# A gated HGRN2 and S5 block on one core: the small matmuls of an S5 slot gathered in one group

## The chip, the cores and the metric

The kernel runs on one core of a Trainium2 chip. The metric is the device time of one execution in microseconds, as the median of several runs. The names of the engines are those of the profile: PE is TensorE (its weight loads are PEld), DVE is VectorE, ACT is ScalarE, POOL is GpSimd, and SP issues DMAs.

## What is computed

Input x is 2048 tokens of 1024 channels. `u = RMSNorm(x)` is projected to eight parts. Two mixers run beside each other, gates merge them, and a second gated projection and a last norm follow. The S5 mixer, cut to its core:

```python
# 32 groups of 16 channels, each with 64 complex states
xr = einsum('bsgc,gnc->bsgn', u, bbr);  xi = einsum('bsgc,gnc->bsgn', u, bbi)
hr, hi = associative_scan(lam * h + x)             # over the sequence
y  = C_re hr - C_im hi + d * u
ys = gelu(y); ys = glu_a * sigmoid(glu_b) * silu(z)
h += W_out(sigmoid(gate_hg) * y_hg + sigmoid(gate_s5) * y_s5)
h += (p @ W_ple) * sigmoid(RMSNorm(h) @ W_ple_gate)
return RMSNorm(h)
```

## The kernel before

Three parts follow each other on every engine: the head (norm, the projections of HGRN2 and its mixer), the S5 part (`part_s5`) and the tail (`part_tail`). Every large product is made of three float32r matmuls (`split_matmuls`, L107 to L109): weights and activations are each split in a rounded value and the rest, by ACT (the rounding) and DVE (the difference). `u_hi` and `u_lo` stay in SBUF.

The S5 part has NB = 20 slots. In slot b, PE projects weight block b over four token tiles (`project`, 8 x 3 matmuls of 512 columns for each tile). The first four blocks are z slots: DVE multiplies each drained tile (`gated`). The other blocks are gates, drained by a sigmoid on ACT. POOL stores the tiles. Beside this, slots 2 to 17 hold the S5 work of one pair of groups each, p = b - 2.

The S5 work of a pair cuts the sequence in 256 chunks of 8 tokens. `matrices` (DVE) builds bb, X and Z. PE turns X through bank `px` (transposes, L1123), and ACT copies the result to `w_in_t` (L1192). PE makes the taps, the response within a chunk, from bb and Z (L1127); DVE's `taps` copies them to `msb`, and SP spreads them by eight DMAs in `w_intra` (L1053). PE makes the inputs of each chunk from `w_in_t` and U into `pin` (L1138). DVE's `angles` and ACT's Sin make the rotations, and DVE's `states` rotates the inputs, scans them and writes `Hp`. Last, PE makes the outputs from `w_intra` and U (L1146), and from Z and Hp (L1150), into `py`; ACT's `gelu` drains them, and POOL's `store_y` writes them to memory. Within a slot PE has transposes and taps inside the second tile of the projection, the inputs inside the third tile, and the outputs behind the fourth. All these small matmuls are plain float32; they have two records each in the profile, the transposes one.

Engines run their instructions in order, with semaphore waits written out by hand. DVE's order in a slot is `matrices`, `angles`, (z: `gated` 0), the difference of the next slot's weights (L1212), `taps`, (`gated` 1), `states`, (`gated` 2 and 3). ACT's order is `gelu` of the pair before, Sin, the copy to `w_in_t`, and the four drains, with the rounding of the next weights (L1164) behind the first. SP's order is weights, U of the next pair (behind the outputs of the pair before), and the eight copies of the taps.

The tail has the sections glu, os5, ohg, out, ple and pgate, in units of one weight load. Blocks go round six PSUM banks. Two means of squares are needed for each token tile: DVE adds eight squares in `sumsq` [128, 512] (L1892), and one float32 matmul with ones adds them over the partitions (`mean_square`, L1663), behind the first unit of glu, and behind that of os5. `one_over_rms` on ACT follows. In the last tile there is only the first of these, inside ple, and the very last mean is made in two halves (L1738). The head has such a matmul too, but in float32r (L479): it first adds the upper 64 partitions to the lower ones, and puts the rounded sum in the lower half of `osq_parts` and the rest in the upper half.

Of the kernel before, what the change touches and what calls it, by code (L numbers as in the profile page):

```python
# [18 lines left out]
ds = bass.ds  # L19
# [100 lines left out]
def part_head(nc, c, a, w, banks, xs, u_hi, u_lo):  # L120
# [9 lines left out]
    with Bufs(nc, "hg") as m:  # L130
# [818 lines left out]
        return Part(sync, gpsimd, tensor, scalar, vector, drained=[(sigf, STEPS), (sg_done, STEPS), (iv_staged, 2 * TOKENS), (qe_done, STEPS)],  # L949
# [3 lines left out]
def part_s5(nc, c, a, w, banks, u_hi, u_lo, drained, head_over):  # L953
# [11 lines left out]
    with Bufs(nc, "s5") as m:  # L965
# [19 lines left out]
        Z = m.sb("Z", [P, 2, SC + 1, GC])  # L985
# [10 lines left out]
        ps, py, px, pin = banks[0:NT], banks[4:6], banks[6], banks[7]  # L996
# [10 lines left out]
        def slots(engine, body):  # L1007
# [6 lines left out]
            for b in range(PAIRS, NB):  # L1014
                body(b, b - AHEAD if b < PAIRS + AHEAD else None, b % 2, False)
# [3 lines left out]
        def sync(sp):  # L1019
# [13 lines left out]
            def body(b, p, r, z):  # L1033
# [12 lines left out]
                if not is_at(p, 0):  # L1046
                    sp.wait_ge(y_done, p)
                if not isinstance(p, int) or p + 1 < PAIRS:
                    load_u(p + 1, 1 - r)
                sp.wait_ge(msb_done, p * 2 + 2)  # L1050
                for j in range(SC):
                    rows = slice(j * GC, (j + 1) * GC)
                    sp.dma_start(w_intra[rows, r, :, j * GC:P], msb[:, :, 0:SC - j].rearrange("c q j d -> c q (j d)")  # L1053
                                 ).then_inc(intra_in, 16)
# [3 lines left out]
        def gpsimd(pool):  # L1058
# [19 lines left out]
            def body(b, p, r, z):  # L1078
                if is_at(b, 1):
                    constants()  # L1080
                if p is not None and not is_at(p, 0):
                    store_y(p - 1, 1 - r)
                elif is_at(b, PAIRS + AHEAD):
                    store_y(PAIRS - 1, 1)
                for t in range(NT):
# [8 lines left out]
        def tensor(pe, last_step):  # L1094
# [13 lines left out]
            def body(b, p, r, z):  # L1108
                pe.wait_ge(w_lo_done, b + (W0 + 1))
                first = is_at(p, 0)  # L1110
                if p is None:
                    for t in range(NT):
                        project(b, r, t)
                        if is_at(b, 0):
                            last_step(t)
                    return
                project(b, r, 0)
                project(b, r, 1, range(0, 3))
                if not first:
# [12 lines left out]
                pe.wait_ge(turned_done, p + 1)  # L1132
                pe.wait_ge(u_in[r], (p // 2) * 32 + 32 if isinstance(p, int) else (p - r) * 16 + 32)
                if not first:
                    pe.wait_ge(hp_done, p)
                for k in range(2):
                    for q in range(2):
                        ins = pe.matmul(pin[q * NS:(q + 1) * NS, k * NCK:(k + 1) * NCK], w_in_t[:, k, q * NS:(q + 1) * NS],  # L1138
                                        U[:, r, q], start=True, stop=True)
                ins.then_inc(pin_done, 1)  # L1140
                project(b, r, 2, range(2, KT))
                project(b, r, 3)
                pe.wait_ge(intra_in, (p + 1) * 16 * SC)
# [990 lines left out]
```

## Time and profile before

| | |
|---|---|
| median of 3 runs | 2202.24 us (2201.95 to 2203.3) |
| the profiled execution: its own time | 2201.22 us |
| its span | 2199.6 us |
| granted TensorE clock, mean | 0.998 |
| busy: PE, PEld | 2182.7 us (99%), 1782.0 us (81%) |
| busy: DVE, ACT, POOL | 1371.7 us (62%), 941.7 us (43%), 148.2 us (7%) |
| PE's longest waits | 1.8 us (L1738), 1.7 us (L380), 1.6 us (L107 at the start), 0.6 us (L1123) |

The span runs from the first to the last instruction of one execution. A matmul of 512 columns in float32r has a record of 0.39 us, but the next one starts 0.23 us after it: the records overlap, and what a matmul costs is read from the distance of starts.

### The profile page before, as it was taken

What the parts mean: (1) busy time and instruction counts of PE and PEld (TensorE: products, weight loads), DVE (VectorE), ACT (ScalarE), POOL (GpSimd) and SP (SyncE); (2) the same over time, 40 slices, a digit from 0 to 9 for tenths busy, and PEclk for the clock granted to TensorE, in tenths of its full rate; (3) what the DMA queues carried; (4) which work ended last, traced back from release to release, by engine and by line L of the source; (5) the groups of instructions that cost most, each with busy time, mean ns of one, the idle gap of its engine ahead of it and who ended that gap; (6) DMA issues with size and microseconds to landing.
All of it is one profiled execution on the core that took longest, in us unless ns stands there. A gap on an engine that the chain in (4) does not pass through costs nothing.

```text
span 2199.6 us, 29498 instructions
## 1 busy us (share of the span) xinstructions
PE 2182.7 (99%) x10488; PEld 1782.0 (81%) x10488; DVE 1371.7 (62%) x2788; ACT 941.7 (43%) x1381; POOL 148.2 (7%) x268
## 2 busy tenths in 40 slices
PE   9999999999999999999999999999999999999997
PEld 7788888888888888887777777888888888888886
DVE  7700058778778778757666566266567566665756
ACT  6511145545545555533333333243444354354345
POOL 0000000000000000011111111111002001200100
PEclk9999999999999999999999999999999999999999
DMA  6422111111111111022222222376347536634632
GB/s 220 105 72 67 48 63 58 37 41 57 42 39 53 43 38 43 25 92 85 82 83 88 85 85 80 95 225 187 116 123 244 169 97 189 226 111 128 226 116 77
DMA packets 140092, 223.25 MB, mean 101 GB/s; under 512 B 38816, under 2 KB 82592, under 8 KB 140000
## 3 DMA queue, kind: packets, MB, share of 16 engines
q1 hardware_dynamic: 119920, 160.39, 24.2%
q0 software_dynamic: 20080, 61.64, 8.0%
q8 instruction: 57, 0.93, 0.2%
q14 instruction: 35, 0.29, 0.0%
HBM read 166.25 MB, written 54.53 MB: 100 GB/s over the span
## 4 chain that ended last, share of the span: by engine, by line
PE 96%; DVE 2%; ACT 1%; DMA 1%; issue 0%; SPq 0%; DVEq 0%; ACTq 0%
PE c_bank L107 30%; PE c_bank L108 29%; PE c_bank L109 29%; PE c_bank L474 1%; PE c_bank L451 1%; PE c_bank L461 1%; PE c_bank L472 1%; PE c_bank L1150 1%; PE c_bank L1138 1%; PE c_bank L1146 1%; PE c_bank L1127 0%; PE c_bank L479 0%; DMA x_xs<-x_in 0%; PE c_bank L1663 0%; DVE x_xs L824 0%
## 5 line engine op out<-in xcount | busy, mean ns | idle before, releaser
L107 PE MATMUL c_bank<-u_hi,c_w_both 128*128 128x512 f32 x1216 | 487.0, 400 | 2.8 <-DVE c_w_both L880 1.6
L109 PE MATMUL c_bank<-u_hi,c_w_both 128*128 128x512 f32 x1216 | 473.5, 389 | 0.0
L108 PE MATMUL c_bank<-u_lo,c_w_both 128*128 128x512 f32 x1200 | 468.3, 390 | 0.0
L107 PEld LDWEIGHTS c_bank<-u_hi,c_w_both 128*128 128x128 f32 x1216 | 228.3, 188 | 71.6 <-issue 20.6
L109 PEld LDWEIGHTS c_bank<-u_hi,c_w_both 128*128 128x128 f32 x1216 | 228.3, 188 | 48.8
L108 PEld LDWEIGHTS c_bank<-u_lo,c_w_both 128*128 128x128 f32 x1200 | 225.5, 188 | 42.9 <-issue 0.2
L1744 ACT ACTIVATE c_w_both<-c_raw 128x1024 fp32r<-128x1024 f32 x90 | 95.4, 1060 | 179.8 <-PE c_bank L109 169.4
L721 DVE STREAM_TRANSPOSE hg_ken<-hg_ke 32x128 f32<-32x128 f32 x512 | 154.8, 302 | 6.5
L1197 ACT ACTIVATE s_stage<-c_bank 128x512 f32<-128x512 f32 x80 | 47.6, 596 | 207.5 <-PE c_bank L109 182.8
L109 PE MATMUL c_bank<-t_oa_hi,c_w_both 128*128 128x512 f32 (+1 forms) x344 | 132.1, 384 | 0.0
L108 PE MATMUL c_bank<-t_oa_lo,c_w_both 128*128 128x512 f32 (+1 forms) x344 | 132.1, 384 | 0.0
L107 PE MATMUL c_bank<-t_oa_hi,c_w_both 128*128 128x512 f32 (+1 forms) x344 | 132.1, 384 | 0.0
L1874 DVE TENSOR_TENSOR c_w_both<-c_raw,c_w_both 128x1024 fp32r<-128x1024 f32 x90 | 109.8, 1220 | 16.1 <-ACT c_w_both L1744 16.1
L541 ACT ACTIVATE hg_S<-hg_G,hg_coef 128x128 f32<-128x128 f32 x120 | 47.5, 401 | 158.1 <-DVE hg_G L746 112.1
L107 PE MATMUL c_bank<-u_hi,hg_wq 128*128 128x512 f32 x256 | 102.3, 400 | 0.0
L108 PE MATMUL c_bank<-u_lo,hg_wq 128*128 128x512 f32 x256 | 99.8, 390 | 0.0
L109 PE MATMUL c_bank<-u_hi,hg_wq 128*128 128x512 f32 x256 | 99.7, 389 | 0.0
L108 PE MATMUL c_bank<-n_iv_w_lo,u_hi 128*128 128x512 f32 x256 | 99.6, 389 | 0.0
L1744 ACT ACTIVATE t_w_hi<-c_raw 128x1024 fp32r<-128x1024 f32 x45 | 47.8, 1061 | 88.1 <-PE c_bank L109 81.1
L1212 DVE TENSOR_TENSOR c_w_both<-c_raw,c_w_both 128x1024 fp32r<-128x1024 f32 x19 | 23.3, 1226 | 91.5 <-ACT c_w_both L1164 91.5
L535 ACT ACTIVATE n_iv_stage<-c_bank 128x512 f32<-128x512 f32 x32 | 19.0, 597 | 133.6 <-PE c_bank L109 131.6
L108 PEld LDWEIGHTS c_bank<-t_oa_lo,c_w_both 128*128 128x128 f32 x344 | 64.6, 188 | 12.9
(334 smaller groups left out, 4557.9 us busy)
## 6 DMA issues: line engine op xcount, KB each, us to landing
c_raw<-w_in_in SPq DMA_DIRECT2D x44, 512.0 KB, 4.0
gates_scratch<-s_stage POOLq DMA_DIRECT2D x64, 256.0 KB, 2.7
t_ein<-gates_scratch SPq DMA_DIRECT2D x64, 256.0 KB, 4.4
c_raw<-w_o_hg_in SPq DMA_DIRECT2D x32, 512.0 KB, 3.9
c_raw<-w_out_in SPq DMA_DIRECT2D x32, 512.0 KB, 3.6
c_raw<-w_ple_gate_in SPq DMA_DIRECT2D x32, 512.0 KB, 3.6
iv_rows_scratch<-n_iv_stage SPq DMA_DIRECT2D x32, 256.0 KB, 2.3
hg_ivn<-iv_rows_scratch SPq DMA_DIRECT2D x32, 256.0 KB, 2.8
```

The costliest lines, as they stand in the source:

```text
L107: pe.matmul(out, w_hi, u_hi, start=first, stop=False)
L108: pe.matmul(out, w_hi, u_lo, start=False, stop=False)
L109: return pe.matmul(out, w_lo, u_hi, start=False, stop=last)
L451: pe.matmul(psc[0:CH, both], ke[:, p, 0], qe[:, p, 0:2].rearrange("p a j -> p (a j)"), start=True, stop=True)
L461: ins = pe.matmul(pk[:, p * P:(p + 1) * P], ken[:, p], ivn[:, t % 2, p], start=True, stop=True)
L472: pe.matmul(po[:, at], S[:, p], qe[:, p, 0:2].rearrange("p a j -> p (a j)"), start=True, stop=False, skip_group_check=True)
L541: act.activation(S[:, p], G[:, (p + 1) % 2], ACT.Copy, scale=coef[:, 2 * p:2 * p + 1]).then_inc(states, 1)
L721: ins = dve.transpose(ken[j * SQ:(j + 1) * SQ, :, i * SQ:(i + 1) * SQ], ke[i * SQ:(i + 1) * SQ, :, 1 + j // 2, j % 2 * SQ:(j % 2 + 1) * SQ])
L1197: act.activation(stage[:, t], ps[t][:], ACT.Sigmoid).then_inc(sig_done if z else staged, 1)
L1212: dve.tensor_tensor(w_lo[:, r], raw[:, r], w_hi[:, r].bitcast(F32), ALU.subtract).then_inc(w_lo_done, 1)
L1744: act.activation(w_hi[u % WS], raw[u % RS], ACT.Copy).then_inc(w_hi_done, 1)
L1874: dve.tensor_tensor(w_lo[u % WS], raw[u % RS], w_hi[u % WS].bitcast(F32), ALU.subtract).then_inc(w_lo_done, 1)
```

## The change

It does the following.

- S5, PE: a slot projects its four tiles first. Behind them stands one group: inputs and taps of pair p, then the outputs of pair p - 1, of which Z and Hp come first and `w_intra` last. Pair 15's outputs move to slot 18. Z has two buffers for this. The PE transposes and bank `px` go.
- S5, DVE: `turn_inputs` turns X by sixteen 32x32-block transposes, each for both parts (32 x 2 x 32). The order becomes `taps` of pair p - 1, `matrices` of p, (`gated` 0), weights, `states` of p - 1, (`gated` 1), `turn_inputs`, (`gated` 2), `angles`, (`gated` 3).
- S5, ACT, POOL and SP: the copy to `w_in_t` goes; gelu and the store of y come a slot later, gelu behind the taps; U is loaded in the slot that uses it; the copies of msb stand ahead of the slot's group.
- Tail: six means of squares (all but the last tile's) are made as in the head: ACT lifts the upper half to `sq`, DVE adds it, ACT rounds, DVE takes the difference, and one float32r matmul sums `sq_parts`. The matmul moves behind the first block of the section's second unit.

```diff
@@ part_s5, sync
-                if not is_at(p, 0):
-                    sp.wait_ge(y_done, p)
-                if not isinstance(p, int) or p + 1 < PAIRS:
-                    load_u(p + 1, 1 - r)
-                sp.wait_ge(msb_done, p * 2 + 2)
+                if not isinstance(p, int) or p >= 2:
+                    sp.wait_ge(y_done, p - 1)
+                if not is_at(p, 0) and not is_at(p, PAIRS):
+                    load_u(p, r)
+                if is_at(p, 0):
+                    return
+                sp.wait_ge(msb_done, p * 2)
...
@@ part_s5, tensor
             def body(b, p, r, z):
                 pe.wait_ge(w_lo_done, b + (W0 + 1))
-                first = is_at(p, 0)
+                for t in range(NT):
+                    project(b, r, t)
+                    if is_at(b, 0):
+                        last_step(t)
                 if p is None:
-                    for t in range(NT):
-                        project(b, r, t)
-                        if is_at(b, 0):
-                            last_step(t)
                     return
-                project(b, r, 0)
-                project(b, r, 1, range(0, 3))
-                if not first:
-                    pe.wait_ge(gelu_done, p)
-                pe.wait_ge(xz_done, p + 1)
-                for q in range(2):
-                    pe.transpose(px[:, q * P:(q + 1) * P], X[:, q].rearrange("p j c -> p (j c)"), c["ident"][:])
-                for q in range(2):
-                    rows = slice(q * NS, (q + 1) * NS)
+                if not is_at(p, 0):
+                    pe.wait_ge(hp_done, p)
+                if not is_at(p, PAIRS):
+                    pe.wait_ge(xz_done, p + 1)
+                    pe.wait_ge(turned_done, p + 1)
+                    pe.wait_ge(u_in[r], (p // 2) * 32 + 32 if isinstance(p, int) else (p - r) * 16 + 32)
                     for k in range(2):
-                        ins = pe.matmul(py[q][0:GC, NCK:NCK + P], bb[rows, k],
-                                        Z[rows, k, 0:SC].rearrange("p j c -> p (j c)"), start=k == 0, stop=k == 1)
-                ins.then_inc(mats_done, 1)
-                project(b, r, 1, range(3, KT))
-                project(b, r, 2, range(0, 2))
-                pe.wait_ge(turned_done, p + 1)
-                pe.wait_ge(u_in[r], (p // 2) * 32 + 32 if isinstance(p, int) else (p - r) * 16 + 32)
-                if not first:
-                    pe.wait_ge(hp_done, p)
-                for k in range(2):
+                        for q in range(2):
+                            ins = pe.matmul(pin[q * NS:(q + 1) * NS, k * NCK:(k + 1) * NCK], w_in_t[:, k, q * NS:(q + 1) * NS],
+                                            U[:, r, q], start=True, stop=True)
+                    ins.then_inc(pin_done, 1)
                     for q in range(2):
...
+                        rows = slice(q * NS, (q + 1) * NS)
+                        for k in range(2):
+                            ins = pe.matmul(py[q][0:GC, NCK:NCK + P], bb[rows, k],
+                                            Z[rows, r, k, 0:SC].rearrange("p j c -> p (j c)"), start=k == 0, stop=k == 1)
+                    ins.then_inc(mats_done, 1)
+                if is_at(p, 0):
+                    return
+                pe.wait_ge(intra_in, p * 16 * SC)
+                if not is_at(p, 1):
+                    pe.wait_ge(gelu_done, p - 1)
                 for k in range(2):
                     for q in range(2):
                         rows = slice(q * NS, (q + 1) * NS)
...
+                        pe.matmul(py[q][:, 0:NCK], Z[rows, 1 - r, k, 1:SC + 1].rearrange("p j c -> p (j c)"),
+                                  Hp[rows, k], start=k == 0, stop=False)
+                for q in range(2):
+                    ins = pe.matmul(py[q][:, 0:NCK], w_intra[:, 1 - r, q], U[:, 1 - r, q], start=False, stop=True)
                 ins.then_inc(y_done, 1)
@@ part_s5, scalar
-                if is_at(b, PAIRS + AHEAD):
+                if is_at(b, NB - 1):
                     gelu(PAIRS - 1, 1)
...
+                elif not isinstance(b, int) or b >= AHEAD + 2:
+                    act.wait_ge(msb_done, p * 2)
+                    gelu(p - 2, r)
+                if p is not None and not is_at(p, 0):
+                    act.wait_ge(ang_done, p)
                     act.activation(trig[:], trig[:], ACT.Sin, scale=TWO_PI).then_inc(trig_done, 1)
-                    act.wait_ge(mats_done, p + 1)
-                    act.activation(w_in_t[:].rearrange("p k n -> p (k n)"), px[:, 0:2 * P], ACT.Copy).then_inc(turned_done, 1)
@@ part_s5, vector
+                def turn_inputs():
+
+                    rows = X[:].rearrange("p k j c -> p k (j c)")
+                    for i in range(P // SQ):
+                        for j in range(P // SQ):
+                            ins = dve.transpose(w_in_t[j * SQ:(j + 1) * SQ, :, i * SQ:(i + 1) * SQ],
+                                                rows[i * SQ:(i + 1) * SQ, :, j * SQ:(j + 1) * SQ])
+                    ins.then_inc(turned_done, 1)
...
@@ part_tail, tensor
-                pe.matmul(ms[which][:], c["ones"][:].bitcast(F32), sumsq[:], start=True, stop=True).then_inc(ms_done, 1)
+                if t == NT - 1:
+                    pe.matmul(ms[which][:], c["ones"][:].bitcast(F32), sumsq[:], start=True, stop=True).then_inc(ms_done, 1)
+                else:
+                    pe.wait_ge(sum_lo_done, STEPS + 2 * t + which + 1)
+                    pe.matmul(ms[which][:], c["ones"][:], sq_parts, start=True, stop=True).then_inc(ms_done, 1)
...
-                if body and sec == "glu" and i == 0:
-                    mean_square(0, t, None if first else t * 2)
-                if body and not last and sec == "os5" and i == 0:
-                    mean_square(1, t, None if first else t * 2)
+                        if body and i == 1 and bl == 0 and sec in ("glu", "os5"):
+                            mean_square(("glu", "os5").index(sec), t, None if first else t * 2)
@@ part_tail, scalar
+            def lift_sums(which, t):
+                act.wait_ge(summed, t * 16 + 8 * which + 8)
+                act.activation(sq[low], sumsq[up], ACT.Copy).then_inc(up_done, 1)
+
+            def round_sums(which, t):
+                act.wait_ge(folded, STEPS + 2 * t + which + 1)
+                act.activation(sq_parts[low], sumsq[low], ACT.Copy).then_inc(sum_hi_done, 1)
@@ part_tail, vector
+            def fold_sums(which, t):
+                n = 2 * t + which
+                dve.wait_ge(up_done, 2 * STEPS + n + 1)
+                dve.tensor_tensor(sumsq[low], sumsq[low], sq[low], ALU.add).then_inc(folded, 1)
+                dve.wait_ge(sum_hi_done, STEPS + n + 1)
+                dve.tensor_tensor(sq_parts[up], sumsq[low], sq_parts[low].bitcast(F32), ALU.subtract).then_inc(sum_lo_done, 1)
```

## Rows read from the trace of the kernel before

**Rows 1.** The page's busy times and its chain that ended last, by engine.
```profile
PE 2182.7 (99%) x10488; PEld 1782.0 (81%) x10488; DVE 1371.7 (62%) x2788; ACT 941.7 (43%) x1381; POOL 148.2 (7%) x268
...
PE 96%; DVE 2%; ACT 1%; DMA 1%; issue 0%; SPq 0%; DVEq 0%; ACTq 0%
```

**Rows 2.** Timeline of PE, one S5 slot: start, duration, engine, line, op, tiles.
```profile
1214.64 0.39 PE L109 MATMUL c_bank<-u_hi,c_w_both 128*128 128x512 f32 x1
...
1220.31 0.38 PE L1123 MATMUL c_bank<-c_ident,s_X 128*128 128x128 f32 x2
1220.62 0.62 PE L1127 MATMUL c_bank<-s_Z,s_bb 64*16 64x128 f32 x8
1221.17 0.50 PE L107 MATMUL c_bank<-u_hi,c_w_both 128*128 128x512 f32 x1
1221.51 0.39 PE L108 MATMUL c_bank<-u_lo,c_w_both 128*128 128x512 f32 x1
...
1225.84 0.39 PE L109 MATMUL c_bank<-u_hi,c_w_both 128*128 128x512 f32 x1
1226.16 1.08 PE L1138 MATMUL c_bank<-s_U,s_w_in_t 128*64 128x256 f32 x8
1227.17 0.50 PE L107 MATMUL c_bank<-u_hi,c_w_both 128*128 128x512 f32 x1
...
1236.87 1.02 PE L1146 MATMUL c_bank<-s_U,s_w_intra 128*128 128x256 f32 x4
1237.83 1.13 PE L1150 MATMUL c_bank<-s_Hp,s_Z 64*128 64x256 f32 x8
1238.89 0.50 PE L107 MATMUL c_bank<-u_hi,c_w_both 128*128 128x512 f32 x1
```

**Rows 3.** Timeline of PE, the first and the last group of S5.
```profile
983.15 0.39 PE L109 MATMUL c_bank<-u_hi,c_w_both 128*128 128x512 f32 x1
984.13 0.44 PE L1123 MATMUL c_bank<-c_ident,s_X 128*128 128x128 f32 x2 [0.59 <-DVEq L1300]
...
1396.39 0.40 PE L108 MATMUL c_bank<-u_lo,c_w_both 128*128 128x512 f32 x1
```

**Rows 4.** Timeline of PE at a mean of squares, and L479 by form.
```profile
1575.70 1.02 PE L1663 MATMUL c_bank<-t_sumsq,c_ones 128*128 128x512 f32 x2
...
1576.80 0.40 PE L108 MATMUL c_bank<-t_ya_lo,c_w_both 128*128 128x512 f32 x1
...
L479 PE MATMUL c_bank<-hg_osq_parts,c_ones 128*128 128x512 f32 x32 | 12.5, 390 | 0.0
```

**Rows 5.** Timeline of DVE, one S5 slot.
```profile
1239.16 0.23 DVE L1282 TENSOR_SCALAR s_mt<-s_bim,s_si 128x16 f32 x1 [4.07 <-PE c_bank L1150]
...
1245.01 0.35 DVE L1304 TENSOR_SCALAR s_t<-s_nn,s_f_hi 128x256 f32<-128x256 f32 x1 [0.24 <-DVE s_Z L1298]
...
1252.49 1.23 DVE L1212 TENSOR_TENSOR c_w_both<-c_raw,c_w_both 128x1024 fp32r<-128x1024 f32 x1 [3.83 <-ACT c_w_both L1164]
...
1254.28 0.41 DVE L1329 TENSOR_TENSOR s_xt<-c_bank,s_trig 128x256 f32<-128x256 f32 x1
...
1260.85 0.42 DVE L1343 TENSOR_TENSOR s_Hp<-s_Hp,s_t 128x255 f32<-128x255 f32 x1
```

**Rows 6.** Timeline of DVE in the head: its sixteen transposes of one step.
```profile
705.91 5.04 DVE L721 STREAM_TRANSPOSE hg_ken<-hg_ke 32x128 f32<-32x128 f32 x16
```

**Rows 7.** Timeline of ACT, the same S5 slot.
```profile
1240.37 0.66 ACT L1171 ACTIVATE s_ysb<-c_bank 128x256 f32<-128x256 f32 x2
...
1249.62 1.28 ACT L1197 ACT_TABLE_LOAD   x1
```

**Rows 8.** SP's loads of y for the tail: timeline, and issues with landing.
```profile
1405.13 3.98 SPq L1549 DMA_DIRECT2D t_xa<-ys_scratch  x4
...
t_xa<-ys_scratch SPq DMA_DIRECT2D x4, 256.0 KB, 5.2
```

**Rows 9.** Timeline of DVE in the tail: the last add of a sum.
```profile
1572.07 0.69 DVE L1892 TENSOR_TENSOR t_sumsq<-t_sumsq,t_sq 128x512 f32<-128x512 f32 x1 [0.85 <-ACT t_sq L1760]
```

More of the change, by code:

```diff
@@ L1259, in parameters, with pair @@
                 par(dve.tensor_tensor(si[:], si[:], den[:], ALU.mult))
-            LINKS = 38
-            def pair(p, r, first):
+            LINKS, AHEAD_OF_IT = 38, 24
+            def pair(p, r):
                 n = [0]
@@ L1279, in matrices @@
                     flat = lambda x: x[:, pc].rearrange("p a c -> p (a c)")
-                    if not first:
-                        dve.wait_ge(y_done, p)
+                    if not is_at(p, 0) and not is_at(p, 1):
+                        dve.wait_ge(y_done, p - 1)
                     link(dve.tensor_scalar(mt[:, 0], flat(bim), si[:, pc], None, ALU.mult))
@@ L1343, in states @@
                     link(dve.tensor_tensor(Hp[:, 1, 1:], Hp[:, 1, 1:], t2[:, 0:last], ALU.add))
-                    assert n[0] == LINKS
                     dve.sem_inc(hp_done, 1)
-                return matrices, angles, taps, states
+                return matrices, turn_inputs, angles, taps, states
             def gated(b, t):
@@ L1352, in body @@
             def body(b, p, r, z):
+                make = p is not None and not is_at(p, PAIRS)
+                use = p is not None and not is_at(p, 0)
                 if p is not None:
-                    matrices, angles, taps, states = pair(p, r, is_at(p, 0))
+                    matrices, turn_inputs, angles, taps, states = pair(p, r)
+                if use:
+                    taps()
+                if make:
                     matrices()
-                    angles()
                 if z:
@@ L1366, in body @@
                     tail_inputs()
-                if p is not None:
-                    taps()
+                if use:
+                    states()
                 if z:
@@ L1372, in body @@
                         last_step(1)
-                if p is not None:
-                    states()
+                if make:
+                    turn_inputs()
                 if z:
-                    for t in (2, 3):
-                        gated(b, t)
-                        if b == 0:
-                            last_step(t)
+                    gated(b, 2)
+                    if b == 0:
+                        last_step(2)
+                if make:
+                    angles()
+                if z:
+                    gated(b, 3)
+                    if b == 0:
+                        last_step(3)
             slots(dve, body)
@@ L1787, in unit @@
                     x = tile(sec, t, j, body)
+                    if body and sec == "os5" and i == 0 and bl == 0:
+                        lift_sums(1, t)
+                        round_sums(1, t)
                     if sec == "glu" and bl == 0:
+                        if body and i == 0:
+                            lift_sums(0, t)
                         act.wait_ge(filled[x.bank], x.use + 1)
@@ L1918, in unit @@
                     while_rounded()
+                if body and i == 0 and sec in ("glu", "os5"):
+                    fold_sums(("glu", "os5").index(sec), t)
                 blocks = KT // KTS[sec]
@@ L2040, in build @@
             s5 = part_s5(nc, c, a, w, banks, u_hi, u_lo, head.handed_on["drained"], head.handed_on["over"])
-        tail = part_tail(nc, c, a, w, banks, s5.handed_on)
+        tail = part_tail(nc, c, a, w, banks, s5.handed_on, head.handed_on["fold"])
         block = m.block()
```

65 lines of the change are left out of this document (29 added, 36 removed).

## The prediction

> **What bounds the kernel.** The page's busy table and the chain that ended last come first [rows 1]: TensorE (PE) is busy for 2182.7 us of a span of 2199.6, and 96% of the chain is PE. The reader is to see that nothing counts here but the time that PE spends on instructions plus the few places where it waits. Then the PE timeline of one slot of the S5 stage [rows 2] and of the tail [rows 4] shows what the touched matmuls cost: the start-to-start time of the projection's matmuls is the ruler (25 steps from 1214.64 to 1220.31, 0.2267 us each), and whatever stands between two of them beyond that is the price of the small ones. Last comes the order of work on VectorE (DVE) and ScalarE (ACT) [rows 5 to 7], since PE's group will now wait for a chain of theirs.
>
> **S5, the price now.** From the projection matmul at 983.15 (the 33rd of slot 2) to the one at 1396.39 (the 2nd of slot 18) [rows 3] lie 16 x 96 - 33 + 2 = 1505 steps of 0.2267 us, 341.1 us. 413.2 us passed, so the small matmuls and their waits cost 72.1 us in 16 slots. One wait of 0.59 us for the matrices of the first pair is in it [rows 3].
> In one slot [rows 2]: two transposes from 1220.31 to 1220.62, 0.31 us; eight records of taps to 1221.17, 0.55; then L107 takes 0.34 until L108, 0.11 more than its step. Inputs: due at 1225.84 + 0.23 = 1226.07, begun at 1226.16 (0.09), until 1227.17, 1.01, and again 0.11. Outputs: 0.96 from w_intra and 1.06 from Z and Hp, until 1238.89, and 0.11. Sum 4.31. 72.1 less the wait is 4.47 for a slot; the other 0.16 are slightly slow steps behind each group and a late first w_intra.
>
> **S5, the price after.** Slot p holds one group: inputs and taps of pair p, outputs of pair p-1. The transposes leave PE. The small products themselves stay: 1.01 + 0.55 + 1.06 + 0.96 = 3.58. The entry, 0.09, stays once. Whether a group that ends with the full-height w_intra matmuls costs 0.11 at its exit is read from the tail: there 512 float32 columns over the whole array take from 1575.70 to L108 at 1576.80 [rows 4], 1.10 us with L107's step in it, so 0.87 with entry and exit, while the 512 columns of w_intra took 0.96 ahead of Z. So a full-height part beside the projection has no visible exit, and the group is worth 3.67 (no exit) to 3.83 (exit 0.11 and 0.05 of slow steps). Not shown are the tiled forms directly behind each other: inputs, taps, Z. Bounds: w_intra at 0.87 in place of 0.96 is 3.58; two more changes at 0.16 each on 3.83 (inputs and Z pass 512 columns' worth too, two tiles side by side, and have 0.14 and 0.19 above 0.87) are 4.15. I take 3.76, between the two readings of the exit, nearest to the rows' own sum.
> Three special slots: slot 2 has inputs and taps only, 0.09 + 1.01 + 0.55 + 0.16 = 1.81; slot 18, which had nothing, has outputs only, 0.09 + 1.06 + 0.96 = 2.11; fifteen slots have all. After: 15 x 3.76 + 3.92 = 60.3 us. The gain is 11.8 us (14.5 at 3.58, 5.9 at 4.15). The wait of 0.59 and the late first w_intra are in it: both are now needed only after the slot's whole projection.
> The Trainium skill (TensorEngine Tiling (Array Packing), Tiling Modes, Key Properties) says that changing the tiling mode drains the engine, while changing the tile does not. By that rule a slot goes from six mode changes to four, and w_intra beside the projection changes none; the trace agrees in that the exit is 0.11 behind the tiled forms and not visible behind the full one. At 0.11 for each change the sum would be by this rule 2 x 0.11 + 0.31 = 0.53 for a slot, about 9 us in all.
>
> **S5, does the group wait?** It stands behind all four projections, 96 x 0.2267 = 21.8 us after the former group. Count from that group's end. VectorE sees it 0.27 later (L1282 at 1239.16 behind 1238.89). Taps: 0.6 (from the split of the weights at 1252.49 to L1329 at 1254.28 are 1.79, of which the split takes 1.2) [rows 5]. Matrices 5.85 (1239.16 to 1245.01), so to 6.7. Then the split waits for ACT. ACT waits for the taps at 0.9, then three table loads of 1.28 with gelu (0.66) and a Sin of about the same between [rows 7], to 6.1; the first projection is out by 5.7. The split followed the start of that sigmoid by 1.59 (1249.62 + 1.28 = 1250.90 to 1252.49) [rows 5, 7], so it runs from 7.7 to 8.8. The states take 7.0 (1254.28 to the end of L1343, 1261.27), to 15.8, which gives Hp. Then sixteen transposes of 32x64. No row shows that size: sixteen of 32x128 take 5.04 us [rows 6], so 5.04 is one end; half of it, 2.5, the other. I take 3.2, nearer to half since the data is half. turned_done comes at 18.3 to 20.8, against 21.8: no wait. Angles take the rest, 3.65 (1245.01 to the 3.83 of idle time ahead of 1252.49), to at most 24.5 of a slot of 25.5; DVE had 4.07 us idle ahead of L1282 and 3.83 ahead of the split [rows 5], and these pay for the transposes. In slot 3, a z slot, one drain of 0.7 comes ahead of the transposes: 21.5 at worst, still hidden.
> DMAs: SP's two loads of U now stand at the slot's start, and the eight copies of msb behind the taps, ahead of the group by over 10 us. POOL's store of y moves by one slot.
> The y of pair 15 is ready a slot later. In the last slot, whose 21.8 us hold only projections, it has to pass gelu, POOL's store and SP's four loads before ACT rounds it, behind the second projection's sigmoid, so from 11.5 us on. Table load and gelu are 1.9 [rows 7], the store with its landing is put at no more than the 5.2 at which the loads of the same array land, the loads take 4.0 to issue and 5.2 to land [rows 8]: the last at 16.3, and with rounding and difference of about 1.1 each by 18.5. PE needs it at 21.8. Cost nothing; without that cover the wait would come once, not in each slot.
>
> **Tail.** A mean of squares costs 1.10 - 0.23 = 0.87 us over L107's step [rows 4]. One float32r matmul from folded sums, the form that the head has, has a mean of 390 ns [rows 4], the 0.39 of every projection matmul [rows 2]; so it costs a step, 0.23. Six of seven change (the one of the last tile stays): 6 x 0.64 = 3.9 us. Ends: 3.5 if the neighbours' steps slow a little, 4.1 with the slow steps behind each gone.
> Cover: the last add is at 1572.07 + 0.69 = 1572.8 [rows 9], VectorE splits weights until 1573.9, then lift, fold, rounding and difference, each 0.6 to 0.7 us, end at about 1576; PE asks at 1575.70 + 2.72 = 1578.4, since the matmul moved behind half a unit more. ACT rounds weights and r first, as before, and finds the sums soon after. For the second mean (os5) the same chain has 8.2 us, and the inputs of ohg are split up to 2.7 us later in the first of four units, which the idle ACT makes good. Cost nothing. Uncovered, what the fold overruns is paid six times.
>
> **Sum.** 11.8 + 3.9 = 15.7 us off the span of 2199.6: 2183.9. The profiled execution's own time is 2201.22, 1.6 more than its span, so 2185.5; the median of the runs is 2202.24, 1.0 above that time: 2186.5.
>
> **Rivals.**
> 1. The turned inputs come late. For: DVE gets 3.2 to 5.0 us more in a chain with 1.0 to 3.5 us to spare. Against: the chain as summed from rows 5 to 7. Slower than before: with the gain of 15.7 us spread over 15 slots, each slot would have to wait 1.05 us. So the transposes would have to take 5.04 + 1.0 + 1.05 = 7.1 us, 0.44 each, more than a transpose of double size, 0.315 each. At 0.60 each (15.8 + 9.6 = 25.4, against 21.8) PE waits 3.6 a slot, 54 us, less the gain: 2240.
> The Trainium skill (VectorE: DVE Perf Modes, Rules for kernel authors) advises TensorE for a 128x128 transpose, which speaks against moving it to VectorE. Whether it holds depends on which engine is short, and here the trace shows it to be PE.
> 2. The forms do not like each other: four dense changes at 0.35 each instead of about 0.16. A group is then 4.3 to 4.5 and the gain 0.7 to 3.7 + 3.9: 2195 to 2198. For: the entry of 0.09 and exits of 0.11 show that changes cost. Against: taps came directly behind transposes, and Z behind w_intra, at no visible gap.
> 3. The change does not do what it says: the waits inside the group stop PE. The groups save only the transposes, 16 x 0.31 = 5.0, and the tail 3.9: 2193.3.
> 4. The tail's fold comes late and PE waits for it, while S5 gains: at 0.64 us each time the tail's gain is gone, 2190.4, and the whole is slower only from 15.7 / 6 = 2.6 us each time. Against: 2.4 us to spare in glu.
>
> **Chances.** Forecast and its bounds (gains of 9.4 to 18.6 us, 2183.6 to 2192.8) 0.80; rival 3 or 4, 0.07; rival 2, 0.06, half of it within 0.2%; rival 1, 0.07. 0.2% is 4.4 us, about what a measurement of this kernel can tell from no change. Faster 0.88, same 0.04, slower 0.08. Range 2183 to 2193.5.
>
> **What would show it.** In the changed profile one PE group in each slot, with L109, then the inputs, taps, Z, w_intra, L107, 3.7 to 3.8 us in all; slot period 25.5 instead of 26.2; no wait for w_in_t; transposes near 0.2 us; the tail's mean of squares one record of 390 ns in six places. Wrong if PE waits for w_in_t or Hp in the loop, or if the group is over 4.2 us.

## The result, and the profile after

The changed kernel takes 2184.76 us, median of four runs (2184.3 to 2185.05), beside 2202.09 us (2200.61 to 2203.3) for the kernel before: a ratio of 0.9921 [0.9909, 0.9933], 17.3 us less. The profiled execution has an own time of 2184.62 us, a span of 2183.0 and a mean granted clock of 0.998. Span against span it is 16.6 us less, where the sum had 15.7.

The page's busy times, and its chain that ended last by engine:

```profile
PE 2167.8 (99%) x10450; PEld 1778.6 (81%) x10450; DVE 1437.7 (66%) x3056; ACT 944.8 (43%) x1377; POOL 148.4 (7%) x268
...
PE 98%; DVE 1%; ACT 1%; issue 0%; DMA 0%; DVEq 0%; SPq 0%; ACTq 0%
```

Beside [rows 1]: PE is busy 14.9 us less, DVE 66.0 us more, and the span follows PE. What PE still waits for (us in total, times, longest):

```profile
PE c_bank L1757 <- DVE t_sumsq L2014: 1.9, 1, 1.9
PE c_bank L380 <- POOL c_restart L331: 1.7, 1, 1.7
PE c_bank L107 <- DVE u_lo L829: 0.9, 4, 0.2
PE c_bank L107 <- DVE c_w_both L880: 0.7, 1, 0.7
```

None stands in an S5 group or at a changed mean of squares, and the 0.59 us of [rows 3] are gone. The last row is a wait at the head, in code that the change does not touch. It was 1.6 us in the profile of before, and between 0.7 and 2.0 us in all the profiles below. So about 1 us between any two profiles says nothing about an edit; what an edit does is read within the S5 part or the tail.

**One slot.** The timeline of PE, with the next slot's group as its last row:

```profile
1224.61 0.39 PE L109 MATMUL c_bank<-u_hi,c_w_both 128*128 128x512 f32 x1
1224.93 1.08 PE L1126 MATMUL c_bank<-s_U,s_w_in_t 128*64 128x256 f32 x8
1225.94 0.62 PE L1132 MATMUL c_bank<-s_Z,s_bb 64*16 64x128 f32 x8
1226.49 1.13 PE L1143 MATMUL c_bank<-s_Hp,s_Z 64*128 64x256 f32 x8
1227.56 1.13 PE L1146 MATMUL c_bank<-s_U,s_w_intra 128*128 128x256 f32 x4
1228.34 0.58 PE L107 MATMUL c_bank<-u_hi,c_w_both 128*128 128x512 f32 x1
1228.75 0.39 PE L108 MATMUL c_bank<-u_lo,c_w_both 128*128 128x512 f32 x1
...
1250.42 0.87 PE L1126 MATMUL c_bank<-s_U,s_w_in_t 128*64 128x256 f32 x6
```

The group begins 0.09 after it is due (1224.61 + 0.23 = 1224.84). Then come 1.01 for the inputs, 0.55 for the taps, 1.07 for Z and Hp and 0.78 for w_intra, and L107 takes 0.41 until L108, 0.18 over its step. That is 3.68 us. The period is 1250.42 - 1224.93 = 25.49, less 96 x 0.2267 = 21.76, so the group is worth 3.73; the other 0.05 are slightly slow steps behind it. Beside [rows 2], each small product costs what it did: w_intra had 0.96 in front of Z, and now has 0.78 + 0.18 = 0.96 in front of the projection. What is gone are the transposes (0.31), the three late L107 behind a tiled form, that is, one that uses a part of the array (3 x 0.11), and 0.11 of slow steps.

**Where the time came from.** The tail's first projection matmul, in the kernel before:

```profile
1439.70 0.39 PE L107 MATMUL c_bank<-t_ya_hi,c_w_both 128*128 128x512 f32 x1
```

and the same one in the changed kernel:

```profile
1427.21 0.39 PE L107 MATMUL c_bank<-t_ya_hi,c_w_both 128*128 128x512 f32 x1
```

It comes 12.49 us earlier. Of that, 0.23 is there already at the head's first L479 (312.98 before, 312.75 after), so S5 gives about 12.3 us. The tail gives 16.6 - 12.5 = 4.1 us.

**The chain behind the group.** DVE, from the taps behind the slot's group to the transposes:

```profile
1228.83 0.26 DVE L1325 COPY s_msb<-c_bank 16x112 f32<-16x112 f32 x1 [1.19 <-PE c_bank L1146]
...
1237.17 1.22 DVE L1206 TENSOR_TENSOR c_w_both<-c_raw,c_w_both 128x1024 fp32r<-128x1024 f32 x1 [2.09 <-ACT c_w_both L1159]
...
1244.90 0.42 DVE L1349 TENSOR_TENSOR s_Hp<-s_Hp,s_t 128x255 f32<-128x255 f32 x1
1245.47 3.98 DVE L1301 STREAM_TRANSPOSE s_w_in_t<-s_X 32x64 f32<-32x64 f32 x16
```

The transposes end at 1249.45 (1245.47 + 3.98), and PE's group begins at 1250.42: 0.97 us to spare, at the lower edge of the 1.0 to 3.5 predicted. The sixteen take 3.98 us, 0.249 each, where 3.2 was taken; per transpose that is 79% of the 0.315 of one twice as large [rows 6]. DVE's idle time at the start of this work fell from 4.07 (ahead of L1282) to 1.19 (ahead of the taps, which now come first), and that ahead of the split of the weights from 3.83 to 2.09 [rows 5]: this is what paid.

ACT in the same slot shows the other thing that is late:

```profile
1233.07 0.63 ACT L1186 ACTIVATE s_trig<-s_trig 128x512 f32<-128x512 f32 x1
1234.30 1.28 ACT L1191 ACT_TABLE_LOAD   x1 [0.60 <-PE c_bank L109]
...
1236.09 1.05 ACT L1159 ACTIVATE c_w_both<-c_raw 128x1024 fp32r<-128x1024 f32 x1
```

ACT is free at 1233.70, but the sigmoid's table load begins only at 1234.30, when the first projection is out: it stands behind that wait, not ahead of it. So the split on DVE begins 8.83 after the end of the group (1237.17 - 1228.34), not 7.7.

**The tail.** The difference on DVE, last of the fold's four operations, and the matmul:

```profile
1562.71 0.69 DVE L1933 TENSOR_TENSOR t_mb_hi<-t_sumsq,t_mb_hi 64x512 fp32r<-64x512 f32 x1 [0.70 <-ACT t_mb_hi L1781]
...
1565.93 0.39 PE L1684 MATMUL c_bank<-t_mb_hi,c_ones 128*128 128x512 f32 x1
1566.16 0.39 PE L107 MATMUL c_bank<-t_ya_hi,c_w_both 128*128 128x512 f32 x1
```

The matmul takes one step of 0.23, against 1.10 less L107's step in [rows 4]. The sums are ready at 1563.40, 2.5 us before PE asks (2.4 predicted). Only the first of the three means in glu has so much room. At the second it is 1751.35 - 1749.60 = 1.75 us:

```profile
1748.91 0.69 DVE L1933 TENSOR_TENSOR t_mb_hi<-t_sumsq,t_mb_hi 64x512 fp32r<-64x512 f32 x1 [1.49 <-ACT t_mb_hi L1781]
...
1751.35 0.39 PE L1684 MATMUL c_bank<-t_mb_hi,c_ones 128*128 128x512 f32 x1
```

At the second mean (os5) there is less still, and less than the prediction assumed:

```profile
1640.23 0.69 DVE L1933 TENSOR_TENSOR t_mb_hi<-t_sumsq,t_mb_hi 64x512 fp32r<-64x512 f32 x1 [0.70 <-ACT t_mb_hi L1781]
...
1642.32 0.39 PE L1684 MATMUL c_bank<-t_mb_hi,c_ones 128*128 128x512 f32 x1
```

Ready at 1640.92, asked for at 1642.32: 1.4 us to spare. The third mean in glu has 1.75 again, and each in os5 has 1.4.

### The profile page after: what moved, and what is told of

Read it like the earlier page. It is cut to its first block, busy times and chain, and to the rows that moved or that the text cites. A ratio compares the mean times of both kernels' runs of the same rounds, so it can differ in the third digit from the quotient of the medians.

```text
span 2183.0 us, 29682 instructions
## 1 busy us (share of the span) xinstructions
PE 2167.8 (99%) x10450; PEld 1778.6 (81%) x10450; DVE 1437.7 (66%) x3056; ACT 944.8 (43%) x1377; POOL 148.4 (7%) x268
## 4 chain that ended last, share of the span: by engine, by line
PE 98%; DVE 1%; ACT 1%; issue 0%; DMA 0%; DVEq 0%; SPq 0%; ACTq 0%
PE c_bank L107 30%; PE c_bank L109 30%; PE c_bank L108 30%; PE c_bank L474 1%; PE c_bank L451 1%; PE c_bank L461 1%; PE c_bank L472 1%; PE c_bank L1143 1%; PE c_bank L1146 1%; PE c_bank L1126 1%; PE c_bank L1132 0%; PE c_bank L479 0%; DVE x_xs L824 0%; DVE n_sumsq L846 0%; DVE t_h L2059 0%
## 5 line engine op out<-in xcount | busy, mean ns | idle before, releaser
L107 PE MATMUL c_bank<-u_hi,c_w_both 128*128 128x512 f32 x1216 | 484.6, 399 | 1.8 <-DVE u_lo L829 0.9
L108 PE MATMUL c_bank<-u_lo,c_w_both 128*128 128x512 f32 x1200 | 467.5, 390 | 0.0
L107 PEld LDWEIGHTS c_bank<-u_hi,c_w_both 128*128 128x128 f32 x1216 | 228.3, 188 | 57.8 <-issue 5.9
L108 PEld LDWEIGHTS c_bank<-u_lo,c_w_both 128*128 128x128 f32 x1200 | 225.5, 188 | 44.4 <-issue 0.2
L108 PE MATMUL c_bank<-t_oa_lo,c_w_both 128*128 128x512 f32 (+1 forms) x344 | 132.1, 384 | 0.0
L107 PE MATMUL c_bank<-t_oa_hi,c_w_both 128*128 128x512 f32 (+1 forms) x344 | 132.1, 384 | 0.0
L1908 DVE TENSOR_TENSOR c_w_both<-c_raw,c_w_both 128x1024 fp32r<-128x1024 f32 x90 | 109.7, 1219 | 13.2 <-ACT c_w_both L1763 13.2
L107 PE MATMUL c_bank<-u_hi,hg_wq 128*128 128x512 f32 x256 | 102.3, 400 | 0.0
L108 PE MATMUL c_bank<-u_lo,hg_wq 128*128 128x512 f32 x256 | 99.8, 390 | 0.0
L108 PE MATMUL c_bank<-n_iv_w_lo,u_hi 128*128 128x512 f32 x256 | 99.6, 389 | 0.0
L108 PEld LDWEIGHTS c_bank<-t_oa_lo,c_w_both 128*128 128x128 f32 x344 | 64.6, 188 | 12.9
L109 PEld LDWEIGHTS c_bank<-t_oa_hi,c_w_both 128*128 128x128 f32 x344 | 64.6, 188 | 12.8
```

Of the source, the lines that this page charges most:

```text
L107: pe.matmul(out, w_hi, u_hi, start=first, stop=False)
L108: pe.matmul(out, w_hi, u_lo, start=False, stop=False)
L109: return pe.matmul(out, w_lo, u_hi, start=False, stop=last)
L1908: dve.tensor_tensor(w_lo[u % WS], raw[u % RS], w_hi[u % WS].bitcast(F32), ALU.subtract).then_inc(w_lo_done, 1)
```

## Experiments

Edits are to the changed kernel unless said otherwise. The edits ran in three groups, the kernel before with each (2201.54, 2201.37 and 2201.33 us). The changed kernel did not run again with them, and beside its own runs the kernel before took 2202.09. So a difference between an edit and the changed kernel is uncertain by a further 0.6 to 0.8 us, and the prices below rest on the traces as well.

**s5_only: the S5 part alone.** The tail is that of before.

```diff
-                if t == NT - 1:
-                    pe.matmul(ms[which][:], c["ones"][:].bitcast(F32), sumsq[:], start=True, stop=True).then_inc(ms_done, 1)
-                else:
-                    pe.wait_ge(sum_lo_done, STEPS + 2 * t + which + 1)
-                    pe.matmul(ms[which][:], c["ones"][:], sq_parts, start=True, stop=True).then_inc(ms_done, 1)
+                pe.matmul(ms[which][:], c["ones"][:].bitcast(F32), sumsq[:], start=True, stop=True).then_inc(ms_done, 1)
...
```

> The changed kernel with the tail of before, so the S5 part alone is changed. Theory A (the parts add up, each worth what its matmuls show): 2184.8 + 6 x 0.64 to 0.7 = 2188.8, or 12 to 13.5 us under the kernel before. Theory B (gathering is worth little and the tail's shorter matmuls, with what follows them, the larger share): above 2193.

Measured: 2189.05 us (2188.32 to 2190.11), ratio 0.9944 [0.993, 0.9957]; 12.5 us less than before.

**tail_only: the kernel before with the changed tail.** The edit is the tail's part of the change alone.

```diff
+                    pe.wait_ge(sum_lo_done, STEPS + 2 * t + which + 1)
+                    pe.matmul(ms[which][:], c["ones"][:], sq_parts, start=True, stop=True).then_inc(ms_done, 1)
...
```

> The kernel before with the changed tail alone. Theory A: 2202.1 - 4 = 2198.1, with one record of 390 ns for six means and no new wait of PE. Theory B: under 2195. Theory C (the fold is paid somewhere as a wait, and S5 gave all): 2200 to 2202.

Measured: 2198.11 us (2196.63 to 2199.03), ratio 0.9984 [0.9975, 0.9993]; 3.4 us less than before. The two parts add up to 15.9 us, beside 17.3 for both together, which is within intervals that reach 2 to 3 us to either side of each. The traces say it more closely: from the tail's first projection matmul to the end of the span it is 759.9 us before and 755.9 in tail_only (1440.14 to 2196.0), so the changed tail gives 4.0 us by itself, and in s5_only that matmul stands at 1427.21, as in the changed kernel. Each part gains by itself, and neither spoils the other.

**pe_transposes: X turned on PE again**, between two projection matmuls of the second tile, with ACT's copy behind the second drain, and the rest of the group as it is.

```diff
+                    if t == 1 and p is not None and not is_at(p, PAIRS):
+                        project(b, r, 1, range(0, 4))
+                        pe.wait_ge(xz_done, p + 1)
+                        for q in range(2):
+                            pe.transpose(px[:, q * P:(q + 1) * P], X[:, q].rearrange("p j c -> p (j c)"), c["ident"][:])
+                        project(b, r, 1, range(4, KT))
...
-                if make:
-                    turn_inputs()
```

> The changed kernel, but X is turned on TensorE as before (two float32 transposes behind the fourth k of the second tile, copied to w_in_t by ScalarE behind the second sigmoid); everything else gathered. Theory A (a full-height form beside the projection costs only its own time): 16 x 0.31 = 5.0 us more, about 2189.8. Theory D (each interruption of the projection costs 0.11 at its exit whatever its form): 16 x 0.42 = 6.7 us more. Theory E (the transposes were nothing, gathering gave it all): under 1 us more.

Measured: 2189.77 us (2189.24 to 2189.93), ratio 0.9946 [0.993, 0.9961]: 5.0 us over the changed kernel. PE's timeline, at the transposes of one slot and of the next:

```profile
1214.60 0.38 PE L1117 MATMUL c_bank<-c_ident,s_X 128*128 128x128 f32 x2
1214.73 0.48 PE L107 MATMUL c_bank<-u_hi,c_w_both 128*128 128x512 f32 x1
1215.05 0.40 PE L108 MATMUL c_bank<-u_lo,c_w_both 128*128 128x512 f32 x1
...
1240.50 0.48 PE L107 MATMUL c_bank<-u_hi,c_w_both 128*128 128x512 f32 x1
```

From the transposes to L108 there are 0.45 us with L107's step in them, so 0.22; the period is 1240.50 - 1214.73 = 25.77, 0.28 more than 25.49. Over 16 slots that is 4.5 us, and the wait of the first pair comes back with 0.6. So taking the transposes off PE bought about 5 us, somewhat under a third of the whole.

**two_groups: the outputs apart from the inputs and taps**, behind the fifth of the eight weight blocks of the fourth tile. Nothing else is changed.

```diff
+                    if t == 3 and p is not None and not is_at(p, 0):
+                        project(b, r, 3, range(0, 5))
+                        outputs()
+                        project(b, r, 3, range(5, KT))
```

> The changed kernel with the slot's group cut in two: the outputs (Z, then w_intra) go behind the fifth k of the fourth tile, inputs and taps stay behind the tile; the same matmuls, one interruption more. Theory A: one more entry and one more exit of a tiled form, 0.09 + 0.11 and up to 0.05 of slow steps: 15 slots x 0.2 to 0.25 = 3.0 to 3.8 us more, 2188 to 2188.6. Theory E (interruptions are the whole gain of 12 us, 31 of them): 0.4 each, 6 us more. Theory F (interruptions cost nothing): same time.

Measured: 2188.93 us (2188.17 to 2189.71), ratio 0.9944 [0.9928, 0.9959], 4.2 over the changed kernel. PE's timeline:

```profile
1224.61 0.39 PE L109 MATMUL c_bank<-u_hi,c_w_both 128*128 128x512 f32 x1
1224.92 1.14 PE L1120 MATMUL c_bank<-s_Hp,s_Z 64*128 64x256 f32 x8
1225.99 1.13 PE L1123 MATMUL c_bank<-s_U,s_w_intra 128*128 128x256 f32 x4
1226.77 0.58 PE L107 MATMUL c_bank<-u_hi,c_w_both 128*128 128x512 f32 x1
...
1252.49 0.58 PE L107 MATMUL c_bank<-u_hi,c_w_both 128*128 128x512 f32 x1
```

The period is 1252.49 - 1226.77 = 25.72: a second interruption costs 0.23 us, over fifteen slots 3.5.

**w_intra_between: the same products in another order.** The full-height w_intra now stands between the taps and Z, which are both tiled.

```diff
+                for q in range(2):
+                    pe.matmul(py[q][:, 0:NCK], w_intra[:, 1 - r, q], U[:, 1 - r, q], start=True, stop=False)
                 for k in range(2):
...
-                for q in range(2):
-                    ins = pe.matmul(py[q][:, 0:NCK], w_intra[:, 1 - r, q], U[:, 1 - r, q], start=False, stop=True)
```

> The changed kernel with the outputs in the other order: w_intra (full height) between the taps and Z (both in row halves), Z last; the same matmuls and one interruption, but five changes of form in a group instead of four. Theory J (each change of form costs about 0.1 us): 0.1 to 0.15 us a slot, 16 x that = 1.6 to 2.4 us more. Theory K (only entry and exit of the projection cost, by their own form): Z's exit is 0.11 where w_intra's is 0.18 of which 0.09 was the step over the tail's 0.87, so between 0 and 1 us less or more.

Measured: 2187.76 us (2187.19 to 2189.1), ratio 0.9939 [0.9922, 0.9956], 3.0 over the changed kernel. The slots' first L1126 stand at 1227.28 and 1252.95, a period of 25.67 and 0.18 over 25.49; over the fifteen slots that have all the products it is 2.7. PE's timeline behind the taps:

```profile
1228.84 1.13 PE L1141 MATMUL c_bank<-s_U,s_w_intra 128*128 128x256 f32 x4
1229.90 1.14 PE L1145 MATMUL c_bank<-s_Hp,s_Z 64*128 64x256 f32 x8
1230.96 0.50 PE L107 MATMUL c_bank<-u_hi,c_w_both 128*128 128x512 f32 x1
1231.30 0.40 PE L108 MATMUL c_bank<-u_lo,c_w_both 128*128 128x512 f32 x1
```

w_intra takes 1.06 in place of 0.96, and L107 is 0.11 late behind Z. Neither the products nor the number of interruptions differ, only the changes of form: five in a group in place of four. In the count of forms, two_groups has five too, and before had six. So, counted like this, a change of form costs about 0.2 us here.

The Trainium skill (TensorEngine Tiling (Array Packing), Tiling Modes, Key Properties) has the engine drained at each change of the tiling mode. The runs agree in kind.

At 0.18 to 0.23 for each, the two changes saved and the transposes' 0.28 make 0.64 to 0.74 a slot, and 4.47 - 3.73 = 0.74 was measured. The count takes the taps (64*16) and Z (64*128) as two forms. If they were one, the changed kernel would have three changes, and each edit would add two, at 0.09 to 0.12 each; three changes saved and 0.28 would then make 0.55 to 0.63. No run here separates the two counts. By either count the order of the same products is worth 0.2 us a slot.

**taps_k_outer: the order of the taps' four products.**

```diff
-                    for q in range(2):
-                        rows = slice(q * NS, (q + 1) * NS)
-                        for k in range(2):
+                    for k in range(2):
+                        for q in range(2):
+                            rows = slice(q * NS, (q + 1) * NS)
```

> The changed kernel with the taps' four matmuls ordered as the states' are: both groups' first halves, then both second halves, so that neighbours use different row halves of the array. Theory H (tiles side by side overlap only when neighbours differ): 0.55 us becomes 0.43 to 0.48, 16 slots x 0.07 to 0.12 = 1.1 to 1.9 us less, 2183. Theory I (they overlap already, 0.55 is entry and drain): same.

Measured: 2184.43 us (2184.07 to 2185.42), ratio 0.9922 [0.9908, 0.9935], no difference. In its trace the taps still take 0.55 us (1226.78 to 1227.33): nothing is to be had by alternating the two halves of the array here.

**turns_twice: the transposes doubled**, first into a spare buffer, so 3.98 us more in the chain with 0.97 us to spare.

```diff
+                    for i in range(P // SQ):
+                        for j in range(P // SQ):
+                            dve.transpose(w_spare[j * SQ:(j + 1) * SQ, :, i * SQ:(i + 1) * SQ],
+                                                rows[i * SQ:(i + 1) * SQ, :, j * SQ:(j + 1) * SQ])
```

> The changed kernel with VectorE's sixteen transposes of a slot made twice, the first time into a spare buffer that nothing reads: 3.98 us more in the chain, and no change to the products. In the changed kernel the transposes end 0.97 us ahead of the group. Theory A (the chain taps, matrices, split, states, transposes has that slack and no more): PE waits 3.98 - 0.9 = 3.0 to 3.3 us in each of 15 slots, 2230 to 2234, with the wait in front of the inputs. Theory G (VectorE catches up from its idle time within a slot, since only its sum of busy time counts): 1 us a slot or less, under 2200.

Measured: 2242.39 us (2241.8 to 2242.95), ratio 1.0185 [1.0169, 1.02]. The wait stands where it was expected, in PE's waits:

```profile
PE c_bank L1126 <- DVE s_w_in_t L1305: 41.8, 15, 3.2
```

Eleven of the fifteen are 3.0 to 3.2 us long, the other four 1.7. The time is 8 to 12 us above what was expected. PE's timeline at one such group shows why:

```profile
1260.30 1.30 PE L1126 MATMUL c_bank<-s_U,s_w_in_t 128*64 128x256 f32 x8 [3.19 <-DVE s_w_in_t L1305]
...
1262.50 2.07 PE L1143 MATMUL c_bank<-s_Hp,s_Z 64*128 64x256 f32 x8
```

and its windows (us from and to, their length; PE busy and records; granted clock; DMA share; GB/s), in the group and in the projection behind it:

```profile
1262.00:1265.00 3.00, 3.00 (x16) 0.59 0.00 0
1265.30:1287.00 21.70, 21.70 (x97) 1.00 0.29 88
```

The granted clock falls within the group that follows the wait, to 0.59 over these 3 us; the level is 1.2 GHz for most of them and 2.4 GHz again for the projection. Z, 1.13 in every group of the changed kernel, took 1.47 to 2.08 us in nine of the fifteen slots. Those nine records alone are 6.6 us more. In these nine slots of the S5 part, and in no other, the clock fell. All nine stand behind waits of 3.0 to 3.2 us; behind two such waits (the groups at 1201.22 and 1320.91) and behind the four of 1.7 us it held. From the group at 1201.22 to the next there are 28.74 us, which is the 25.49 and a wait of 3.19. With the clock fallen, it is 30.3 us, 1.6 more. So what a wait costs here is not always the wait alone: the span (2241.3) grew by 58.3 us; 41.8 are waits, 1.2 the head's wait, and 15.3 are the rest, nearly all of it nine times 1.6.

**turns_early: the transposes directly behind the matrices**, ahead of the states instead of behind them.

```diff
                     matrices()
+                    turn_inputs()
...
-                if make:
-                    turn_inputs()
```

> The changed kernel with the transposes moved on VectorE from behind the states to directly behind the matrices, ahead of the split of the weights, where it waits 2.0 to 2.1 us for ScalarE. Theory A: same time, 2184.8, as PE does not wait either way; but 2.0 us of the transposes lie in that idle time, so Hp comes 1.9 us later and w_in_t some 10 us earlier, and the slack of the group rises from 0.97 to about 3.2 us. Rival: the later states or split cost PE a wait, from 0.1 us a slot.

Measured: 2185.4 us (2184.29 to 2186.16), ratio 0.9928 [0.9913, 0.9943]: the same. DVE's timeline has the transposes at 1234.81 to 1238.79, and Hp as the last of the chain:

```profile
1234.81 3.98 DVE L1301 STREAM_TRANSPOSE s_w_in_t<-s_X 32x64 f32<-32x64 f32 x16 [0.16 <-DVE s_Z L1292]
...
1246.53 0.42 DVE L1349 TENSOR_TENSOR s_Hp<-s_Hp,s_t 128x255 f32<-128x255 f32 x1
```

It ends at 1246.95, and PE's group begins at 1249.99: 3.0 us to spare in place of 0.97, since the transposes now fill the 2.09 us for which DVE waited for ACT. Slack that nothing waits for is worth no time, but this order is the safer one.

**early_twice: that order with the transposes doubled.** The edit is those of turns_early and turns_twice together.

> Both at once: transposes early and made twice. Theory A by the slack of 3.2 us: the further 3.98 us leave 0.8 us to wait, 0.7 to 1.2 us in each of 15 slots, 2195 to 2203 in all, and PE waits for Hp and not for w_in_t. Theory G: under 2190.

Measured: 2201.47 us (one run). PE waits in the fifteen slots, and one of the groups shows what follows (two views):

```profile
PE c_bank L1126 <- DVEq L1354: 16.1, 15, 1.8
```

```profile
1262.87 1.08 PE L1126 MATMUL c_bank<-s_U,s_w_in_t 128*64 128x256 f32 x8 [1.22 <-DVEq L1354]
...
1264.44 1.14 PE L1143 MATMUL c_bank<-s_Hp,s_Z 64*128 64x256 f32 x8
```

About 1.1 us of wait a slot (0.3 to 1.8), about what 3.98 less 3.0 gives, and all records at their usual length: behind waits of this size the clock held, and the time is the changed kernel's plus the waits (2184.8 + 16.1 = 2200.9).

**mean_old_place: the folded mean of squares where the old one stood**, half a unit earlier.

```diff
-                        if body and i == 1 and bl == 0 and sec in ("glu", "os5"):
+                        if body and i == 0 and bl == 1 and sec in ("glu", "os5"):
```

> The changed kernel with the tail's six folded means back at the place of before, behind the section's first unit, 2.72 us earlier on TensorE. Theory A (the fold's chain has a length of its own, and the move of the matmul is what hides it): sums are ready 1.4 us ahead of the matmul in os5 and 2.5 us ahead in glu in the changed kernel, so PE would wait 1.3 to 1.5 us at three places and 0.2 to 0.4 at three: 4.5 to 5.7 us more, about 2189.5 to 2190.5, which is the tail's whole gain. Rival (ScalarE and VectorE come earlier if TensorE asks earlier): under 1 us more.

Measured: 2193.62 us (2192.05 to 2193.94), ratio 0.9964 [0.995, 0.9978]: 8.9 us over the changed kernel. PE's waits, and its timeline at one os5 mean:

```profile
PE c_bank L1684 <- DVE t_mb_hi L1933: 6.0, 6, 1.3
```

```profile
1641.29 0.39 PE L109 MATMUL c_bank<-t_za_hi,t_w_lo 128*128 128x512 f32 x1
1642.97 0.47 PE L1684 MATMUL c_bank<-t_mb_hi,c_ones 128*128 128x512 f32 x1 [1.29 <-DVE t_mb_hi L1933]
1643.28 0.40 PE L107 MATMUL c_bank<-t_za_hi,c_w_both 128*128 128x512 f32 x1
```

Due at 1641.52, it begins at 1642.97, 1.45 us late for a wait of 1.29, and takes a step of 0.31 instead of 0.23. So six waits cost 6.0 + 6 x 0.24 = 7.4 us. Of the rest 1.3 is the head's wait, 2.0 us in this profile. The expectation of 4.5 to 5.7 had left out this late start and slow step, and had taken the 2.5 us of room at the first mean in glu for all three. The waits are what the move by 2.72 us takes out of the room that each mean had in the changed kernel: three in os5 of 1.3 (2.72 - 1.4), two in glu of 0.95 (2.72 - 1.75), and 0.17 at the first in glu (2.72 - 2.53). The fold's chain did not come earlier, nor grow: in os5 it is 3.1 us in both kernels, from the end of the last add to that of the difference, with a split of weights inside.

At the old place the fold costs more (7.4 us) than the 3.9 us that it saves. The moved matmul is what makes the tail's part a gain.

## Why the prediction was right, and where its steps were off

**The bound.** PE's occupied time set the end, before and after: spare time of DVE was spent (66 us of it) and the time followed PE's groups.

**S5, the price after.** 3.76 was taken for a group, 3.73 measured, so the S5 part gave about 12.3 us for the 11.8 predicted. The question of whether the group has an exit behind w_intra was put wrongly: L107 is 0.18 late there, more than the 0.11 behind the tiled forms, but w_intra's own start-to-start time is that much shorter. The sum is its old 0.96, not the 0.87 that the tail's float32 matmul suggested as a lower bound. In size, of the 0.74 us of a slot, pe_transposes gives 0.28 to the transposes (0.31 predicted); the rest goes with the two changes of form fewer, priced at 0.23 by two_groups and 0.18 by w_intra_between, where the text had 0.11 for each. The exits themselves were read rightly: three of 0.11 are gone, and with 0.31 of transposes and 0.11 of slow steps they make the 0.74.

**Does the group wait?** No, as predicted, but with less room, and for two mis-sized terms: the transposes took 3.98 and not 3.2, since most of the time of such a transpose does not shrink with its data; and the split of the weights came 1.1 us later, since the sigmoid's table load was counted ahead of ACT's wait and stands behind it. The chain's end, 15.8 + 3.2 = 19.0 behind the former group's end in the prediction, came at 1249.45 - 1228.34 = 21.1, against a group at 22.1. The bounds (18.3 to 20.8) didn't hold that, though their upper end with 1.1 us added would have. The turned inputs were the last thing ready, as the first rival had it.

**The first rival's price.** Its mechanism was shown by turns_twice, in which the chain ran over; its price per microsecond was too low. At waits of 3.0 to 3.2 us it must also pay for a halved clock in nine of the eleven groups behind them, 1.6 us each; at waits of up to 1.8 us (early_twice) it need not. That the clock fell because of the waits was not tried apart from them. **The other rivals.** No wait appeared inside the group, the changes of form cost 0.2 at most and not 0.35, and the tail's fold was in time.

**Tail.** 3.9 us predicted (6 x 0.64 is 3.84), 4.1 between the traces, and by tail_only 3.4 in the medians and 4.0 within its trace. The fold's cover at the first mean in glu was 2.5 us as reckoned (2.4), but 1.75 at the two later ones, for which the text had read no row. In os5 it was 1.4 us, where the text gave the chain "8.2 us" and did not subtract what the chain takes: a step wrong in the text that cost nothing. mean_old_place shows that half a unit less would have cost more than the gain.

**The sum.** 15.7 predicted, 16.6 in the spans. Of the 0.9 between them S5 has 0.5, the tail 0.2, and the head, which the change does not touch, 0.2.

## What to carry to other kernels

Where TensorE sets the end, read the price of small matmuls from starts, not durations, and count how often the form of the array changes: here one more, as counted above, cost about 0.2 us in two different edits, and to order the same products by form costs nothing. Work moved to an idle engine gains only as long as the chain that it joins keeps its slack, so find that chain's last link and its spare time in the new profile, and double the moved work once to learn what lies behind the edge. When an input of a matmul gets a longer chain, move the matmul back by more than that chain, with what else its engines do in between counted in.

## What the runs showed of the hardware

- Sixteen 32x64 float32 transposes on DVE took 3.98 us (0.249 each), and sixteen of 32x128 took 5.04 [rows 6]: half the data, 79% of the time. The same matrices turned on PE cost it 0.22 us, and 0.28 with the slow steps behind.
- One more change of the array's form in a stream of matmuls cost 0.18 (w_intra_between) to 0.23 us (two_groups), if the taps' 64*16 and Z's 64*128 are two forms; half of that if they are one. The first projection matmul behind a tiled form came 0.11 us late.
- ACT's table load of 1.28 us begins only when the wait ahead of its activation is over (1234.30, with ACT idle for 0.60).
- After eleven waits of PE of 3.0 to 3.2 us the granted clock fell nine times within the next group (0.59 over 3 us of one), at 1.6 us each (turns_twice); after four waits of 1.7 us there, and after waits of 0.3 to 1.8 us in early_twice, it never fell.
- A matmul that had waited began 0.16 us later than its wait accounts for, and took a step of 0.31 instead of 0.23 (mean_old_place).
